# A causal mask put on attention scores by VectorE in PSUM, and not by identity matmuls

## The reference, cut to what matters

```
z      = einsum('bhqd,bhkd->bhqk', qi, k) * scale
mask   = key_pos[None, :] < qpos[:, None]
log_1m = where(mask, log_sigmoid(-z), 0.0)
after  = cumsum(log_1m, axis=3, reverse=True) - log_1m
a      = where(mask, exp(log_sigmoid(z) + after), 0.0)
out    = einsum('bhqk,bhkd->bhqd', a, v)
```

## Time and profile before

| | |
|---|---|
| median of three runs | 1664.04 us (1663.41 to 1664.36) |
| the profiled execution, its own time | 1664.42 us |
| its span, first to last instruction | 1662.7 us |
| granted TensorE clock, mean | 1.000 |
| TensorE busy | 1652.6 us |
| VectorE busy | 970.4 us |
| ScalarE busy | 787.7 us |
| GpSimd busy | 72.9 us |

### The profile page before, as it was taken

How to read it: one execution, slowest core, us unless ns; L and a number is a source line. 1 busy time by engine, 2 the same in 40 slices (tenths; PEclk the granted TensorE clock), 3 DMA queues, 4 the chain that set the end, 5 groups by cost and what they waited for, 6 DMA issues and landing times.

```text
span 1662.7 us, 21919 instructions
## 1 busy us (share of the span) xinstructions
PE 1652.6 (99%) x7496; PEld 1372.5 (83%) x7496; DVE 970.4 (58%) x1260; ACT 787.7 (47%) x1115; POOL 72.9 (4%) x65
## 2 busy tenths in 40 slices
PE   8999999999999999999999999999999999999999
PEld 7878888888888888888888888888888888888887
DVE  6888888455554434434648888875545544344344
ACT  6688887333343223223456888863333432232231
POOL 0200000000120000000131000000001100000000
PEclk9999999999999999999999999999999999999999
DMA  5222222323323323322332122223233223223233
GB/s 191 84 82 88 88 76 86 98 94 101 102 89 101 100 89 101 98 92 101 114 128 102 64 89 88 90 71 106 88 101 102 96 94 102 94 96 102 90 100 127
DMA packets 49153, 162.20 MB, mean 98 GB/s; under 512 B 5712, under 2 KB 5968, under 8 KB 49104
## 3 DMA queue, kind: packets, MB, share of 16 engines
q1 hardware_dynamic: 46656, 157.34, 28.5%
q10 hardware_dynamic: 2448, 4.23, 0.7%
HBM read 155.26 MB, written 2.10 MB: 95 GB/s over the span
## 4 chain that ended last, share of the span: by engine, by line
PE 90%; DVE 5%; ACT 2%; DVEq 1%; issue 1%; ACTq 1%; DMA 0%; SPq 0%
PE bank L487 27%; PE bank L488 27%; PE bank L491 27%; PE z L491 1%; PE z L487 1%; PE z L488 1%; PE z L549 1%; PE misc L569 0%; PE misc L566 0%; DVE S L1366 0%; PE z L533 0%; PE z L534 0%; DVE w_lo L1198 0%; DVE t_s L1217 0%; DVE N L1210 0%
## 5 line engine op out<-in xcount | busy, mean ns | idle before, releaser
L487 PE MATMUL bank<-xg_hi,w_hi 128*128 128x512 f32 x1584 | 620.3, 392 | 0.0
L488 PE MATMUL bank<-xg_lo,w_hi 128*128 128x512 f32 x1584 | 617.1, 390 | 0.0
L797 ACT ACTIVATE w_hi<-raw 128x1024 fp32r<-128x1024 f32 (+1 forms) x294 | 302.3, 1034 | 463.9 <-DMA raw<-in_w_units 463.3
L491 PE MATMUL bank<-xg_hi,w_lo 128*128 128x512 f32 x1584 | 391.7, 389 | 0.0
L1198 DVE TENSOR_TENSOR w_lo<-raw,w_hi 128x1024 fp32r<-128x1024 f32 (+1 forms) x294 | 359.1, 1225 | 41.7 <-ACT w_hi L797 22.9
L491 PEld LDWEIGHTS bank<-xg_hi,w_lo 128*128 128x128 f32 x1584 | 297.3, 188 | 61.7
L487 PEld LDWEIGHTS bank<-xg_hi,w_hi 128*128 128x128 f32 x1584 | 297.5, 188 | 61.4
L488 PEld LDWEIGHTS bank<-xg_lo,w_hi 128*128 128x128 f32 x1584 | 297.4, 188 | 61.0
L1203 DVE TENSOR_TENSOR S<-bank,rstd 128x512 f32<-128x512 f32 x152 | 105.0, 690 | 256.6 <-PE bank L491 254.6
L487 PE MATMUL bank<-mid_hi,w_hi 128*128 128x512 f32 x474 | 184.6, 390 | 0.0
L488 PE MATMUL bank<-mid_lo,w_hi 128*128 128x512 f32 x474 | 184.4, 389 | 0.0
(11 more groups left out here) (202 smaller groups left out, 1592.4 us busy)
## 6 DMA issues: line engine op xcount, KB each, us to landing
raw<-in_w_units SPq DMA_DIRECT2D x278, 512.0 KB, 3.3
raw<-in_w_units SPq DMA_DIRECT2D x20, 256.0 KB, 2.9
xT<-in_x SPq DMA_DIRECT2D x8, 256.0 KB, 5.7
mix_hi<-yb_hi ACTq DMA_DIRECT2D x8, 256.0 KB, 2.3
mix_lo<-yb_lo ACTq DMA_DIRECT2D x8, 256.0 KB, 2.4
out_x<-xT SPq DMA_DIRECT2D x7, 256.0 KB, 4.3
ln_g<-in_sgu_ln_g SPq DMA_DIRECT2D x2, 256.0 KB, 4.3
ln_b<-in_sgu_ln_b SPq DMA_DIRECT2D x2, 256.0 KB, 5.0
```

What stands on the lines that cost most here:

```text
L487: mm(dst[:, :], wh[:, k0 + k, :], his[k], start=(k % per == 0), stop=False)
L488: mm(dst[:, :], wh[:, k0 + k, :], los[k], start=False, stop=False)
L491: return mm(dsts[k // per][:, :], wl[:, k0 + k, :], his[k], start=False, stop=(k % per == per - 1))
L797: af(w_hi[at.slot(c)][:, 0:kc, :], raw[at.slot(c)][:, 0:kc, :], ACT.Copy).then_inc(hi_done, 1)
```

## The change

The three matmuls with the identity go. `z_done` is raised by the last score matmul of each `z`. A new step of VectorE, `causal`, waits for `z_done`, takes the minimum of each diagonal block with `limit` in place in PSUM, and raises `z_masked`, for which ScalarE's Abs now waits. `limit` holds 1e30 where the key counts and -1e30 where it does not; it takes the place of `mask_add`. `causal` is called once a head, at four places of VectorE's list: in the last pair behind `split_lo(at, 6)` and ahead of `convolution`; in a looped pair behind `split_lo(at, 6)` and ahead of the second `head_norm`; in a looped pair behind `split_lo(at, 10)` and ahead of `yb_rest`; and ahead of the loop behind `scaled` of unit 0 and its signal, ahead of `softplus_sum`. TensorE's own order is otherwise the same.

```diff
--- before.py
+++ after.py
@@ -143,7 +143,7 @@
         ident = ident_r[:, :].bitcast(F32)
         neg_tri = sb("neg_tri", [P, P], F32R)
         neg_ones = sb("neg_ones", [P, P], F32R)
-        mask_add = sb("mask_add", [P, P], F32R)
+        limit = sb("limit", [P, P])
         rstd = sb("rstd", [P, T])
         sgu_bias = sb("sgu_bias", [P, KC, P])
         sw_hi = sb("sw_hi", [P, KC, P], F32R)
@@ -267,6 +267,7 @@
         v_ok = sem("v_ok")
         slab_in = sem("slab_in")
         z_done = sem("z_done")
+        z_masked = sem("z_masked")
         z_ln = sem("z_ln")
         sp_ok = sem("sp_ok")
         sp_hi = sem("sp_hi")
@@ -400,7 +401,7 @@
 
             nc.gpsimd.memset(S2[:, 0:P], 0.0)
             nc.gpsimd.memset(S0[:, 0:P], -1.0)
-            nc.gpsimd.memset(S1[:, 0:P], 0.0)
+            nc.gpsimd.memset(S1[:, 0:P], -MASKED)
             pool.drain()
 
             triangle(S2[:, 0:P], ALU.not_equal, 1.0, 0, 1, -1)
@@ -531,12 +532,8 @@
                         ks, qs = slice(P * i, P * i + P), slice(P * i, T)
 
                         mm(dst, k_both[:, e, ks], q_twice[:, e, qs], start=(n == 0), stop=False, skip_group_check=True)
-                        mm(dst, k_both[:, e, ks], q_lo[:, e, qs], start=False, stop=False, skip_group_check=True)
-
-                    first = [Z_AT[i] // P for i in blocks]
-                    dst = z[g][:, :].rearrange("p (b q) -> p b q", q=P)[:, first[0]::(first[-1] - first[0]) or NT, :]
-                    mm(dst, ident_r[:, :], mask_add[:, :].rearrange("p (a q) -> p a q", a=1).broadcast_to([P, len(first), P]),
-                       start=False, stop=True, skip_group_check=True).then_inc(z_done, 1)
+                        last = mm(dst, k_both[:, e, ks], q_lo[:, e, qs], start=False, stop=True, skip_group_check=True)
+                    last.then_inc(z_done, 1)
 
             def cumulate(h3, nth):
 
@@ -841,7 +838,7 @@
             def softplus_logs(h3):
 
                 for g, (a, n) in enumerate(S_COLS):
-                    act.wait_ge(z_done, h3 + (g + 1))
+                    act.wait_ge(z_masked, h3 + (g + 1))
                     af(t_s[:, a:a + n], z[g][:, 0:n], ACT.Abs)
                 act.drain()
                 for g, (a, n) in enumerate(S_COLS):
@@ -1210,6 +1207,15 @@
                 stt(dst, N2, 1.5, N1[:, :], ALU.add, ALU.mult).then_inc(chain_done, 1)
                 dve.drain()
 
+            def causal(h3):
+
+                for g, blocks in Z_BLOCKS:
+                    first = [Z_AT[i] // P for i in blocks]
+                    dst = z[g][:, :].rearrange("p (b q) -> p b q", q=P)[:, first[0]::(first[-1] - first[0]) or NT, :]
+                    dve.wait_ge(z_done, h3 + (g + 1))
+                    tt(dst, dst, limit[:, :].rearrange("p (a q) -> p a q", a=1).broadcast_to([P, len(first), P]),
+                       ALU.min).then_inc(z_masked, 1)
+
             def softplus_sum(h3):
 
                 for g, (a, n) in enumerate(S_COLS):
@@ -1301,7 +1307,7 @@
             dve.wait_ge(ident_ok, 1)
             copy(ident_r[:, :], S2[:, 0:P]).then_inc(ident_in, 1)
             copy(neg_tri[:, :], S0[:, 0:P])
-            copy(mask_add[:, :], S1[:, 0:P])
+            copy(limit[:, :], S1[:, 0:P])
             copy(neg_ones[:, :], N0[:, 0:P])
             dve.drain()
             copy(head_ones[:, :], N1[:, 0:P])
@@ -1488,6 +1494,7 @@
                         attention_lo(h3)
                         scaled(at, 3, S2[:, :])
                         split_lo(at, 6)
+                        causal(h3 + 3)
                         convolution()
 
                         softplus_sum(h3 + 3)
@@ -1557,6 +1565,7 @@
                     ya_rest()
                     scaled(at, 7, flat(gates))
                     split_lo(at, 10)
+                    causal(h3 + 6)
                     yb_rest()
 
                     dve.drain()
@@ -1584,6 +1593,7 @@
                 scaled(pl["A"](0), 0, N0[:, :])
                 dve.drain()
                 dve.sem_inc(v_raw, 1)
+                causal(l * 24)
                 softplus_sum(l * 24)
                 fold_sums(l * 8)
                 with dve.Fori(0, PAIRS - 1) as j:
```

## The result

The changed kernel takes 1671.08 us (median of five runs, 1670.64 to 1671.73) against 1663.86 us (five runs, 1663.41 to 1664.36): ratio 1.0044, 95% interval 1.0032 to 1.0055. It is 7.2 us slower. Forecast were 1671.2 us, with a range of 1667.4 to 1676.5.

A forecast was written before the change was run, and what follows sets the result against it. VectorE and ScalarE, waiting on each other, were taken to bound the attention, TensorE the rest. Per layer 3.82 + 0.10 - 0.34 = +3.6 us, two layers +7.2 on 1664.4, median 0.4 lower: 1671.2 us, range 1667.4 to 1676.5.

The forecast's parts named there:

- What paces the attention: Looped attention pairs: VectorE and ScalarE pace each other, TensorE only nearly as slow and waiting some 0.3 us at the squares.
- What is removed: Three identity matmuls a head on TensorE: about 0.34 us a head, 5.4 us for 16 heads if all on the path.
- The price of a mask: Three VectorE operations in PSUM a head: 0.28, 0.42, 0.28 us, in all 0.8; upper bound 1.3 us.
- The first head: A layer's first head: mask stands behind unit 0's scaling, so Abs starts 2.9 us late, in both layers.
- The second head: Second head's mask in looped and last pairs: 0.8 us fits where VectorE idles 1.29 us before newton in the loop; costs nothing.
- The handover: Mask for the next pair's first head, behind a split: Abs 0.55 us late, up to 0.69, three times a layer.
- Where TensorE takes over: Last pair's first cumulate: released 3.82 us later, restart adds 0.1, then TensorE gains 0.34; +3.6 us a layer.
- The clock: Rival: TensorE's clock falls after the first head's long wait, +1.1 to 2.5 us a layer, 1673.4 to 1676.2; 22%.
- one of the signs that I had named for being wrong: Behind the long wait on TensorE: a changed granted clock or matmul spacing would show the forecast wrong.
- the ring: Attention's looped pairs: the loop of VectorE and ScalarE waiting for each other, claimed to set the pace, 55.4 us a pair.
- TensorE's spare time: Looped pairs: TensorE's waits at the first cumulate and the head squares grow by about 1.2 us a pair together.
- The rival on the other side: Whole kernel: TensorE paces after all, so the whole 5.4 us comes off, 1658.6 us; 7%.

The follow-up runs named there:

- experiment 4: Changed kernel with no mask at all, neither matmuls nor minimum, Abs waiting for the last score matmul: 1662.41 us, ratio 0.999 against the kernel before.
- experiment 2: Changed kernel with only the mask of the next pair's first head moved ahead of the split in front of it: 1668.27 us, ratio 1.0024.
- experiment 1: Changed kernel with only the mask of a layer's first head moved early, ahead of the scaling of unit 9: 1664.81 us, ratio 1.0004.
- experiment 8: Changed kernel with the mask of a layer's first head directly ahead of the scaling of unit 0 instead of behind it: 1669.41 us, ratio 1.0031.
- experiment 6: Changed kernel with the second head's mask done twice in the looped pairs, with a drain between: 1671.98 us, ratio 1.005.
- experiment 7: Changed kernel with 15 unread matmuls of 512 columns behind unit 0 of a layer's first pair, filling TensorE's long wait: 1670.49 us, ratio 1.0039.
- experiment 5: Changed kernel with the three matmuls a head put back behind the scores, the minimum kept: 1672.67 us, ratio 1.0053.
- experiment 3: Changed kernel with the first head's mask and the next pair's first-head mask both moved early: 1661.67 us, ratio 0.9985.

## Why the prediction was right, step by step

- *What paces the attention.* Right. The page's 99% would have said a gain of 5.4 us; experiment 4 gives 1.65 for the bare removal, and every move of a mask on VectorE's list moved the time by what it moved Abs, to within some tenths (experiment 2 is 0.9 above its forecast).
- *What is removed.* 0.34 us a head taken, 0.31 measured: from the first score matmul of the second head to the next unit are 98.00 - 96.43 = 1.57 us before and 100.90 - 99.64 = 1.26 after. The whole is then 5.0 us and not 5.4, which changes none of the verdicts.

```profile
96.43 0.40 PE L533 MATMUL z<-q_twice,k_both 128*128 128x512 f32 x1
...
98.00 0.46 PE L487 MATMUL bank<-xg_hi,w_hi 128*128 128x512 f32 x1
```

```profile
99.64 0.39 PE L534 MATMUL z<-q_twice,k_both 128*128 128x512 f32 x1
...
100.90 0.40 PE L488 MATMUL bank<-xg_hi,w_hi 128*128 128x512 f32 x1
```

- *The price of a mask.* 0.289 and 0.421 us measured, 0.28 and 0.42 taken, and three in a row took 0.82. The nearest rows, one from PSUM and one from SBUF, served well.
- *The first head.* 2.9 us forecast. The mask began 0.82 after the scaling's start and not 0.9, and L1248 came 2.21 us later in the trace (88.99 against 86.78), in an execution whose VectorE was 0.60 us earlier at the scaling (76.88 against 77.48): 2.8 us. Experiments 1 and 8 confirm it from two sides.
- *The second head.* Costed at nothing, and it cost nothing, but the reason was only half right. I set its cover by newton's idle time; experiment 6 shows that newton may be late and that Abs is what counts.
- *The handover.* 0.55 us forecast, 0.52 measured, three times a layer.
- *Where TensorE takes over.* At the last pair a wait of 0.17 us before L546 where there was none, and the cumulate started at 257.45 and not at 254.41: +3.0, with the earlier start 3.6, where 3.8 was forecast. In that pair Abs waited 4.62 us and the next step of ScalarE still found 1.33 us of its old 3.06 left, so the mask there was free:

```profile
266.94 1.36 ACT L842 ACTIVATE t_s<-z 128x512 f32<-128x512 f32 x3 [4.62 <-DVE z L1216]
...
272.69 0.60 ACT L885 ACTIVATE N<-misc 64x512 f32<-64x512 f32 x1 [1.33 <-PE misc L566]
```

```profile
257.45 0.47 PE L546 MATMUL z<-s_hi,neg_tri 128*128 128x512 f32 x1 [0.17 <-DVE fold_hl L1248]
```

- *The clock.* The rival came true as an event and not as a cost. I gave it 22% and 1.1 to 2.5 us a layer; the clock fell in both layers, which is one of the signs that I had named for being wrong, but experiment 7 prices it at about 0.6 us in all. What I mis-sized is the slack: I let TensorE's slow stretch be covered by 0.3 us at the squares only. In layer 1 TensorE came to L574 at 99.19, 1.1 us after VectorE would have released it, and the next L1254 still came 55.92 us after the last, no later than in the pairs behind. Nobody on the ring waits for TensorE there for long. In layer 2 the ring was reached twice: Exp came 0.4 us late behind the slow cumulate, and ScalarE waited 0.34 us more for the attention product (L566), which cost another 0.1. The small terms (the last pair's cumulate 0.2 us a layer less late than forecast, 0.1 of it from the first head, and the clock 0.6 in all) cancel; that is luck to within these tenths.
- *TensorE's spare time.* Forecast were waits at L546 and L574 that grow by 1.2 us a looped pair. In a settled pair they are 0.45 (at 201.80) and 0.32 us (at 209.88), and before nothing and up to 0.33: they grew by 0.45. Part of the rest shows at the transposes' weight loads (L515), which waited 0.4 us four times; the whole was not followed. The time does not hang on it, since the ring paces there.

TensorE's timeline at those squares (that row has no wait):

```profile
99.19 0.39 PE L574 MATMUL misc<-sq_hi,head_ones 128*128 128x512 f32 x1
```

- *The rival on the other side* (TensorE paces, 1658.6) fell with experiments 4 and 5.

Open are the 0.9 us that experiment 5 lost beyond the forecast, if they are real, and the tenths of experiments 2 and 4.

## What to carry to other kernels

An engine that is 99% busy need not be the one that sets the pace: look for waits that always follow one other engine at the same lag, and follow the chain through that stage alone. Work taken off it there is worth only what the ring between the other engines leaves, and work put on those engines is paid in full if it stands before the step that the ring goes through. When work moves to an in-order queue, its place on that queue decides: the same three operations, once a layer, cost 6.3 us, or nothing when they were called a few steps earlier.

## What the runs showed of the hardware

A minimum in place in PSUM over 128 and 256 columns takes 0.289 and 0.421 us, within 0.01 us of operations of these widths that write to SBUF (0.283 and 0.415). After TensorE had waited 4.2 us, and also after 3.4 us, its clock was at 1.2 GHz, in layer 1 only from the fourth matmul or so behind the wait and in layer 2 from the first, and was at 2.4 GHz again 4.4 us after work resumed in layer 1 and 5.9 in layer 2. After waits of 1.06 us in the kernel before, and of 1.4 us in experiments 1 and 3, it stayed at 2.4 GHz. The Trainium skill, "TensorE: Matmul & The Clock Gate", section "What's actually happening", says that idleness brings the half rate and activity lifts it; the trace agrees. A fallen clock need not cost its whole slow stretch: here most of it lay where no engine on the ring waited for TensorE, and two falls cost about 0.6 us.
